# Values of the last block as seven half-size products instead of eight, all ahead of the eight heads; heads without value units

## The reference, cut to what matters

```python
def odd_mixer(hc, hl, w_in, decay_logit, w_out, need_ctx):
    q, k, v, g = split(h @ w_in, 4)          # h: 768 x 1024, w_in: 1024 x 4096
    ...                                      # axial rotation of q and k of the latents
    of, ob = retention forward, retention backward over chunks of 128 positions
    o = of + flip(ob)
    o = o * rsqrt(mean(o * o) + EPS)         # per head
    return (o * silu(g)) @ w_out             # latents only
```

## Time and profile before

| | us |
|---|---|
| median of 3 runs (lowest, highest) | 2440.76 (2439.26, 2443.21) |
| the profiled execution, its own time | 2440.05 |
| span of the profiled execution | 2438.8 |
| TensorE busy, of the span | 2294.6 (94%) |
| VectorE busy | 1731.1 (71%) |
| ScalarE busy | 641.6 (26%) |
| mean granted TensorE clock | 0.97 |
| last block from its first fold to the end | 2058 to 2439 |

### The profile page before, as it was taken

One profiled execution on the slowest core, in us unless ns is written; L12 is line 12 of the kernel. 1 busy time (PEld: TensorE's weight loads), 2 busy tenths in 40 slices (PEclk: granted clock), 3 DMA queues, 4 the chain that ended last, 5 costly groups with the idle time before them and its releaser, 6 DMA issues.

```text
span 2438.8 us, 40049 instructions
## 1 busy us (share of the span) xinstructions
PE 2294.6 (94%) x17170; PEld 1710.4 (70%) x17170; DVE 1731.1 (71%) x2924; ACT 641.6 (26%) x1321; POOL 236.2 (10%) x261
## 2 busy tenths in 40 slices
PE   7989989999997999999999989999897998999997
PEld 3676558888883788888756576675765754668973
DVE  3886477887798889878847969789797116774443
ACT  1314241111003311111043344444543312111111
POOL 2000000201541002024400000000000000000000
PEclk9999999999999999999999999999999898999998
DMA  8232335555432233343222101000010032112102
GB/s 336 88 120 88 129 112 173 173 172 171 162 126 77 88 130 130 130 147 133 94 89 83 37 23 36 12 30 22 19 36 20 2 119 76 67 65 70 35 18 103
DMA packets 42368, 227.93 MB, mean 93 GB/s; under 512 B 4752, under 2 KB 4880, under 8 KB 26064
## 3 DMA queue, kind: packets, MB, share of 16 engines
q1 hardware_dynamic: 21600, 140.56, 16.1%
q0 software_dynamic: 20016, 82.72, 10.0%
q10 hardware_dynamic: 576, 2.11, 0.2%
HBM read 219.07 MB, written 6.29 MB: 92 GB/s over the span
## 4 chain that ended last, share of the span: by engine, by line
PE 83%; DVE 12%; ACT 2%; issue 2%; DMA 1%; POOL 0%; ACTq 0%; DVEq 0%; POOLq 0%
PE ps L689 21%; PE ps L2302 10%; PE ps L911 7%; PE ps L3359 5%; PE ps L3549 3%; PE ps L2078 3%; PE ps L1045 2%; PE ps L461 2%; PE ps L1730 2%; PE ps L3744 2%; PE ps L2312 2%; PE ps L2321 2%; PE ps L1086 1%; PE ps L2990 1%; PE ps L3022 1%
## 5 line engine op out<-in xcount | busy, mean ns | idle before, releaser
L2302 PE MATMUL ps<-H,ring 128*128 128x256 f32 (+1 forms) x832 | 271.4, 487 | 5.4 <-ACT LW L2521 2.6
L689 PE MATMUL ps<-right_sums,left_sums 128*128 128x256 f32 x1056 | 242.8, 379 | 2.7 <-DVE left_sums L669 2.7
L2302 PEld LDWEIGHTS ps<-H,ring 128*128 128x128 f32 x832 | 157.4, 190 | 112.8 <-issue 92.8
L689 PEld LDWEIGHTS ps<-right_sums,left_sums 128*128 128x128 f32 x1056 | 200.5, 190 | 30.6 <-DVE left_sums L669 3.5
L689 PE MATMUL ps<-H,ring 128*128 128x256 f32 x704 | 164.2, 385 | 11.4 <-ACT H L632 11.4
L911 PE MATMUL ps<-G,ring 128*128 128x256 f32 x704 | 159.8, 379 | 0.0
L689 PEld LDWEIGHTS ps<-H,ring 128*128 128x128 f32 x704 | 134.6, 192 | 34.2 <-issue 11.5
L911 PEld LDWEIGHTS ps<-G,ring 128*128 128x128 f32 x704 | 133.8, 190 | 18.1
L381 POOL DMA_DIRECT2D ada_late<-ada_rest x104 | 55.9, 538 | 684.5 <-DVE mod L361 372.1
L756 ACT ACTIVATE C<-U,params_sb 128x512 f32<-128x512 f32 x44 | 35.8, 814 | 315.7 <-DVE U L781 315.7
L689 PE MATMUL ps<-H,left_sums 128*128 128x256 f32 x352 | 86.9, 388 | 0.0
(11 more groups left out here) (628 smaller groups left out, 4971.3 us busy)
## 6 DMA issues: line engine op xcount, KB each, us to landing
ada_late<-ada_rest POOLq DMA_DIRECT2D x104, 512.0 KB, 3.8
ring<-w_up SPq DMA_DIRECT2D x44, 1024.0 KB, 4.8
ring<-w_down SPq DMA_DIRECT2D x16, 1024.0 KB, 4.9
ring<-od_in SPq DMA_DIRECT2D x16, 1024.0 KB, 4.9
ring<-ev_in SPq DMA_DIRECT2D x15, 1024.0 KB, 4.8
ada_early<-ada_rest POOLq DMA_DIRECT2D x24, 512.0 KB, 4.8
ada_first_sb<-ada_first SPq DMA_DIRECT2D x7, 1024.0 KB, 16.4
ring<-ab_in SPq DMA_DIRECT2D x7, 1024.0 KB, 6.1
```

The costliest lines, as they stand in the source:

```text
L689: return pe.matmul(product(k, n, j), lhsT[:, i, :], rhs[:, i, :], start=(i == 0), stop=(i == 3))
L2302: mm = pe.matmul(k.ps[:, bank + b, 0:tn], wv[:, kk, (i % 2) * P:(i % 2 + 1) * P], k.H[:, kk, t0:t0 + tn], start=(kk == 0), stop=(kk == DT ...
```

## The change

Folds 11 to 16 are added for the values: folds 11 to 13 make columns 0 to 511 (slabs 12 and 13 together), folds 14 to 16 columns 512 to 1023 (slabs 14 and 15 together). In a fold the input blocks are the array's weights and the slab's blocks (two slabs side by side) the moving operand of 256 columns. All value units are removed; the six folds stand between the gates' folds and head 0. The output products that fill move to heads 3 to 7, always behind the states but for the last pair. The rest of the diff only routes the folds' outputs (`fold_out`: `k.V` for values) and adds the buffer `k.VL` over `k.XA`.

```diff
-FOLDS = [("q", 1), ..., ("g", 3)]
+FOLDS = [("q", 1), ..., ("g", 3)] + [("v", t) for t in range(6)]
...
+def value_fold_first_dve(k, q):
+    v, (A, S) = k.nc.vector, value_fold_left(k, q)
+    for h in range(2):
+        v.wait_ge(*k.when("slab", k.slab("od_in", 12 + 2 * q + h)))
+    v.wait_ge(*(k.when("fold", 13, 5) if q else k.when("fold", 9, 3)))
+    settled(k, v.tensor_tensor(S[0], A[1, 0], A[1, 1], ALU.add))
+    v.tensor_tensor(S[1], S[0], A[0, 0], ALU.subtract).then_inc(*k.says(DVE, "value fold left", q, 6))
+
+def value_fold_last_dve(k, q):
+    v, (A, S) = k.nc.vector, value_fold_left(k, q)
+    v.wait_ge(*(k.when("fold", 13, 7) if q else k.when("fold", 10, 3)))
+    v.wait_ge(*k.when("value fold left", q, 6))
+    v.tensor_tensor(S[3], A[0, 1], S[1], ALU.subtract).then_inc(*k.says(DVE, "value fold left", q, 3))
+    v.tensor_tensor(S[2], A[0, 0], A[1, 0], ALU.subtract).then_inc(*k.says(DVE, "value fold left", q, 7))
+
+def value_fold_pe(k, t):
+    q = t // 3
+    pe, m, (A, S) = k.nc.tensor, 11 + t, value_fold_left(k, q)
+    B, R = fold_right(k, "k")
+    def times(j, left, right):
+        for i in range(4):
+            mm = pe.matmul(fold_ps(k, m, j), right[:, i, (t % 3) * P:(t % 3 + 1) * P], left[:, i, :], start=(i == 0), stop=(i == 3))
+        mm.then_inc(*k.says(PE, "fold", m, j))
+    for h in range(2):
+        pe.wait_ge(*k.when("slab", k.slab("od_in", 12 + 2 * q + h)))
+    pe.wait_ge(*k.when("fold kept", m - 1))
+    times(1, A[0, 0], B[0, 0])
+    pe.wait_ge(*k.when("fold low", m - 1))
+    times(2, A[0, 1], B[1, 0])
+    pe.wait_ge(*k.when("value fold left", q, 6))
+    pe.wait_ge(*k.when("fold base", m - 1))
+    times(6, S[1], R[:, 1])
+    pe.wait_ge(*k.when("fold end", m - 1))
+    times(5, S[0], R[:, 0])
+    pe.wait_ge(*k.when("value fold left", q, 3))
+    times(3, S[3], B[1, 1])
+    pe.wait_ge(*k.when("value fold left", q, 7))
+    times(7, S[2], R[:, 2])
+    pe.wait_ge(*k.when("folded", m - 1))
+    times(4, A[1, 1], R[:, 3])
+    if t % 3 == 2:
+        for h in range(2):
+            k.mark(PE, "slab used", k.slab("od_in", 12 + 2 * q + h))
...
 def odd_gates_dve(k):
     for s in range(4):
         if s < 3:
             fold_left_dve(k, 8 + s)
+        else:
+            value_fold_first_dve(k, 0)
         axial_dve(k, ("od", "k"), k.Kr, TC, 2 * s)
         fold_base_dve(k, 7 + s)
...
         fold_ends_dve(k, 7 + s)
+    value_fold_last_dve(k, 0)
...
 def retention_scores_pe(k, h):
...
+    else:
+        pe.wait_ge(*k.when("fold base" if h == 0 else "folded", 16))
...
 def retention_states_pe(k, h):
-    pe.wait_ge(*k.when("value kept", NC * (h // 2) + NC - 1))
+    pe.wait_ge(*k.when("folded", 16))
...
-EARLY_PRODUCTS = {(6, 0): [(0, kk) for kk in range(4)], (6, 1): [(1, kk) for kk in range(4)], (6, 2): [(0, 4), (1, 4)], (7, 0): [(0, 5), (1, 5)]}
+EARLY_PRODUCTS = {(3, 2): [(0, 0), (1, 0)], (4, 2): [(0, 1), (1, 1), (0, 2)], (5, 2): [(1, 2), (0, 3), (1, 3)], (6, 2): [(0, 4), (1, 4)], (7, 0): [(0, 5), (1, 5)]}
...
 def retention_pe(k):
-    for u in range(NC):
-        value_unit_pe(k, u)
+    for t in range(6):
+        value_fold_pe(k, t)
...
 def retention_dve(k):
+    for t in range(6):
+        fold_base_dve(k, 11 + t)
+        if t == 2:
+            value_fold_first_dve(k, 1)
+        fold_ends_dve(k, 11 + t)
+        if t == 2:
+            value_fold_last_dve(k, 1)
```

More of the change, by code:

```diff
@@ L3296, in axial_dve @@
     v.tensor_tensor(x, x, rot, ALU.add).then_inc(*k.says(DVE, *what, "turned", j))
-FOLDS = [("q", 1), ("q", 2), ("q", 3), ("k", 0), ("k", 1), ("k", 2), ("k", 3), ("g", 0), ("g", 1), ("g", 2), ("g", 3)]
+FOLDS = [("q", 1), ("q", 2), ("q", 3), ("k", 0), ("k", 1), ("k", 2), ("k", 3), ("g", 0), ("g", 1), ("g", 2), ("g", 3)] + [("v", t) for t in range(6)]
 FOLD_FIRST = {"q": -1, "k": 3, "g": 7}
-FOLD_PART = {"q": (0, HALF, TC), "k": (4, 3 * P, 0), "g": (8, HALF, TC)}
+FOLD_PART = {"q": (0, HALF, TC), "k": (4, 3 * P, 0), "g": (8, HALF, TC), "v": (12, 2 * P, 0)}
 FOLD_ORDER = (1, 2, 6, 5, 3, 7, 4)
@@ L3382, in fold_pe, with fold_out @@
     k.mark(PE, "slab used", k.slab("od_in", fold_slab(m)))
+def fold_out(k, m, h, s):
+    what, n = FOLDS[m]
+    if what == "v":
+        return k.V[:, 3 * s + n % 3, (2 * (n // 3) + h) * 2 * P:(2 * (n // 3) + h + 1) * 2 * P]
+    w = FOLD_PART[what][1]
+    return {"q": k.Q, "k": k.Kr, "g": k.Gr}[what][:, 2 * n + h, s * w:(s + 1) * w]
 def fold_kept_act(k, m):
@@ L3396, in fold_base_dve @@
     what, s = FOLDS[m]
-    v, w, O = k.nc.vector, FOLD_PART[what][1], {"q": k.Q, "k": k.Kr, "g": k.Gr}[what]
+    v, w = k.nc.vector, FOLD_PART[what][1]
     p1, x0, x1, x2 = (k.FP[:, j, 0:w] for j in range(4))
@@ L3400, in fold_base_dve @@
     v.wait_ge(*k.when("fold", m, 2))
-    v.tensor_tensor(O[:, 2 * s, 0:w], p1, fold_ps(k, m, 2), ALU.add).then_inc(*k.says(DVE, "fold low", m))
+    v.tensor_tensor(fold_out(k, m, 0, 0), p1, fold_ps(k, m, 2), ALU.add).then_inc(*k.says(DVE, "fold low", m))
     v.wait_ge(*k.when("fold", m, 6))
@@ L3414, in fold_ends_dve @@
     v.wait_ge(*k.now(DVE))
-    v.tensor_tensor(O[:, 2 * s, w:2 * w], x1, fold_ps(k, m, 3), ALU.add).then_inc(*k.says(DVE, "fold high", m))
+    v.tensor_tensor(fold_out(k, m, 0, 1), x1, fold_ps(k, m, 3), ALU.add).then_inc(*k.says(DVE, "fold high", m))
     v.wait_ge(*k.when("fold", m, 7))
     settled(k, v.tensor_tensor(x2, x0, fold_ps(k, m, 7), ALU.add))
-    v.tensor_tensor(O[:, 2 * s + 1, w:2 * w], x2, fold_ps(k, m, 5), ALU.add).then_inc(*k.says(DVE, "fold end", m))
+    v.tensor_tensor(fold_out(k, m, 1, 1), x2, fold_ps(k, m, 5), ALU.add).then_inc(*k.says(DVE, "fold end", m))
@@ L3419, in fold_ends_dve, with value_fold_left @@
     v.wait_ge(*k.when("fold", m, 4))
-    v.tensor_tensor(O[:, 2 * s + 1, 0:w], x2, fold_ps(k, m, 4), ALU.add).then_inc(*k.says(DVE, "folded", m))
-    if what != "g":
+    v.tensor_tensor(fold_out(k, m, 1, 0), x2, fold_ps(k, m, 4), ALU.add).then_inc(*k.says(DVE, "folded", m))
+    if what in "qk":
         for n in range(2):
             k.mark(DVE, "od", what, "kept", 2 * s + n)
+def value_fold_left(k, q):
+    w = [k.slab_view("od_in", 12 + 2 * q + h, DT, 2 * P) for h in range(2)]
+    return {(h, e): w[h][:, e:DT:2, :] for h in range(2) for e in range(2)}, [k.VL[:, (j + 2) % 4] for j in range(4)]
@@ L3747 @@
 ODD_BANKS, ODD_SUM = (3, 7, 0, 1), 5
-EARLY_PRODUCTS = {(6, 0): [(0, kk) for kk in range(4)], (6, 1): [(1, kk) for kk in range(4)], (6, 2): [(0, 4), (1, 4)], (7, 0): [(0, 5), (1, 5)]}
+EARLY_PRODUCTS = {(3, 2): [(0, 0), (1, 0)], (4, 2): [(0, 1), (1, 1), (0, 2)], (5, 2): [(1, 2), (0, 3), (1, 3)], (6, 2): [(0, 4), (1, 4)], (7, 0): [(0, 5), (1, 5)]}
 def fill_pe(k, h, i):
     pe = k.nc.tensor
-    if NC + 3 * h + i < 4 * NC:
-        value_unit_pe(k, NC + 3 * h + i)
-        return
     for n, kk in EARLY_PRODUCTS.get((h, i), ()):
         pe.wait_ge(*k.when("slab", k.slab("od_out", 0)))
-        pe.wait_ge(*k.when("value kept", 4 * NC - 1))
         pe.wait_ge(*k.when("retained", kk))
         odd_product_pe(k, n, kk)
-def fill_act(k, h, i):
-    if NC + 3 * h + i < 4 * NC:
-        value_unit_act(k, NC + 3 * h + i)
 def retention_pe(k):
-    for u in range(NC):
-        value_unit_pe(k, u)
+    for t in range(6):
+        value_fold_pe(k, t)
     for h in range(RH):
@@ L3801, in retention_act @@
     log_exp_act(k)
-    for u in range(NC):
-        value_unit_act(k, u)
+    for t in range(6):
+        fold_kept_act(k, 11 + t)
     for h in range(RH):
@@ L3806, in retention_act @@
             retention_square_act(k, h - 1)
-        fill_act(k, h, 0)
         if h:
             retention_rstd_act(k, h - 1)
-        fill_act(k, h, 1)
-        fill_act(k, h, 2)
     retention_square_act(k, RH - 1)
@@ L3953, in lay_memory @@
     k.RL, k.RA = k.at("fold_right_latents", [P, 4, 4, HALF], values), k.at("fold_right_all", [P, 4, 4, 3 * P], LIMIT // 8 * 8 - 48 * P)
+    k.VL = k.at("value_fold_left", [P, 4, 4, 2 * P], xa)
     k.LF = [k.at(f"fold_left{n}", [P, 4, 4, P], xa + 2048 * n) for n in range(2)]
```

## The result

The changed kernel takes 2463.01 us (median of 4 runs, 2460.20 to 2463.99), the kernel before beside it 2441.99 (4 runs, 2439.26 to 2444.31): **21.0 us slower**, ratio 1.0086, 95% interval 1.0071 to 1.0101. The forecast was 2459.0, 18 us slower, with a range of 2452 to 2466.

A forecast was written before the change was run, and what follows sets the result against it. The prediction took TensorE's matmuls to limit the heads before the change. Its terms, -10.4 + 9.6 + 7.4 + 2.0 + 9.6 = +18.2 us, gave a median of 2459.0 us, with an 8-in-10 range of 2452 to 2466.

The forecast's parts named there:

- The work, -10.4: TensorE's value matmuls: 192 in units become 168 in folds, 24 fewer at 0.432 us each, -10.4 us.
- The seam at fold 11, +9.6: Before fold 11: 4.2 us for the load of slab 13 and 5.4 for VectorE's late sums, +9.6 us.
- the second wait of 1.5 us: In fold 11: TensorE, after product 6, waits again for VectorE's "fold end", about 1.5 us.
- 5.4: At fold 11: the part of the +9.6 us put down to what VectorE does late, 5.4 us.
- The seam at fold 14, +7.4: Before fold 14: slabs 14 and 15 wait for fold 13's end; 7.2 us plus 0.2 for semaphores, +7.4.
- The clock, +2.0: Behind the wait at fold 14: one stretch of some 4 us at half clock, +2.0 us.
- The heads, +9.6: Heads without filling: TensorE idles for walks, squares and head 0's decayed keys, together +9.6 us.
- The tail, 0: Behind the states of head 7: the tail stays the same, 0 us.
- VectorE is not late: Rival at fold 11: only the load counts, 4.2 in place of 9.6 us, 2453.6; chance 0.10.
- The loads come early: Rival at both seams: slabs come before folds 10 and 13 end, seams and clock cost nothing, 2440.0; chance 0.04.
- The waits of the heads are hidden: Rival in the heads: scores and squares overlap better and hide the waits, seams as forecast, 2449.4; chance 0.04.
- The clock falls more often: Rival: half clock also in fold 11's products 2 and 6 (3.5) and once in the heads (2.0), 2464.5; chance 0.17.

The follow-up runs named there:

- profile with filled heads: Changed kernel plus two extra matmuls of 512 columns, result unused, behind the states of heads 0, 1 and 2: 2461.56 us, ratio 1.0086.
- the first experiment: Changed kernel with VectorE's first two sums for the values behind the ends of fold 10 instead of ahead of key tile 6: 2457.53 us, ratio 1.0074.
- the matmuls put in it: Changed kernel with extra unused matmuls where TensorE waits for slabs, 5 ahead of fold 11 and 8 ahead of fold 14: 2459.13 us, ratio 1.0071.
- the one-pair run: Changed kernel without od_in slabs 14 and 15; folds 14 to 16 take slabs 12 and 13 again: 2451.96 us, ratio 1.0048.
- the run with both edits: Changed kernel with VectorE's first value sums behind the ends of fold 10 and without slabs 14 and 15: 2448.38 us, ratio 1.0033.
- the version with units: Against the kernel before: one-slab folds for slabs 12 to 14, slab 15 as six value units in heads 0 to 5: 2434.10 us, ratio 0.9975.

## Why the prediction was right, point by point

- **The work, -10.4**: right. The folds that nothing disturbs take 12.1 us each (12 and 13: 24.2).
- **The seam at fold 11, +9.6**: measured 10.0 (23.0 less 12.1 and the 0.9 of before), but made up otherwise. "TensorE does product 1 of fold 11 from 2225.3 to 2227.0" was too quick: it took 3.6 us at the low clock, beside VectorE's sums and so at no cost, as said. Then the clock was low again behind the wait, in products 2, 6 and the start of 5, 1.8 us, which the prediction had as a bound (3.5) and not in its sum; and this took the place of the second wait of 1.5 us, for "fold end". The profile with filled heads has it the other way round, full clock and a wait of 1.3, with the same end within 0.1. So the two do not add up, and the term came out near the forecast because VectorE's sums set it, not because the path on TensorE was foreseen. That VectorE's order matters is shown by the first experiment (3.8 us in the stretch), that it was less than 5.4 too.
- **The seam at fold 14, +7.4**: the wait was 7.7 us, from fold 13's end to the first product. The pair was in 7.3 us after the first issue.
- **The clock, +2.0**: 2.4 at fold 14, shown to be the wait's doing by the matmuls put in it, and gone with the loads in the one-pair run. The argument that a wait of 2.5 us leaves the clock full was weak, though. The earlier trace rows is the window of the wait itself (behind it the matmuls of the earlier trace rows did run at full pace); the changed kernel reads 1.00 there too, and 0.53 in the window behind. And the kernel before had a counterexample in its gates' folds, a wait of 2.45 us with low clock behind it. In the ten profiles this wait is 2.4 to 2.6 us long, and the product behind it takes 2.6 to 3.7 us in nine of them and runs at full pace in one, the run with both edits (first line before, second line that run):

```profile
2187.47 3.50 PE L3359 MATMUL ps<-fold_right_latents,fold_left 128*128 128x256 f32 x8 [2.45 <-DVE Gr L3418]
2185.08 1.99 PE L3359 MATMUL ps<-fold_right_latents,fold_left 128*128 128x256 f32 x8 [2.63 <-DVE Gr L3427]
```

- **The heads, +9.6**: mis-sized, and the largest of the errors; they took 76.7 where 75.0 was forecast, so the term is 11.3. The prediction gave the row sum 0.86 us; behind its wait for the square it takes 1.12, the same 0.27 that it did count for the output. Six heads wait so, 1.6 us. The first states stand behind a wait as well, for the decayed keys, and take 2.51 in place of 2.23. Heads 1 to 3 took 9.5 where 9.2 was forecast, heads 5 and 6 10.85 where "10 to 11" stood.
- **The tail, 0**: it is 70.6 us in place of 69.3 in this profile, because the clock fell behind the last walk. Whether the change has a part in this is not shown. In the nine profiles with a tail of this form it is 69.1 to 69.3 in five and 70.6 to 70.8 in four, each group with and without seams ahead; but all four have heads without filling, and the two profiles with heads filled throughout (the kernel before and the version with units) are among the five. The walk's wait of 2.5 us sometimes brings the low clock and sometimes not.
- **Together**: the stretch was to grow by 18.2 us and grew by 20.8. The misses are 0.4, 0.3, 0.4 and 1.7 (the heads), all the same way, so none of these terms hides another's error.

Of the rivals, *VectorE is not late* gave 2453.6 and is refuted by TensorE's wait of 2.2 us for a `Gr` sum and by the first experiment. *The loads come early* is refuted: slab 13 was issued 0.2 us behind fold 10's end. *The waits of the heads are hidden* is refuted by the chain. *The clock falls more often* is half right: it fell once more in fold 11's products, for 1.8 and not 3.5 us, and not in the heads. The Trainium skill ("TensorE: Matmul & The Clock Gate", section "HAM oscillation — how this bites in real kernels") has it that bursts of matmuls split by waits on a load can start at the low clock each time. The two waits on loads, of 4.9 and 7.5 us, agree. Behind the wait of 2.2 us on VectorE the clock was low here and full in the profile with filled heads (2.0 us); behind the heads' waits of 0.7 to 1.5 us nothing of it showed up to the states of head 7. The median, 2463.0, lies nearer to this rival's 2464.5 than to the forecast's 2459.0, but the rival's two terms do not make it: the low clock in products 2 and 6 takes the place of a wait, and the heads keep their clock. The miss in the heads is first matmuls behind waits.

## What to carry to other kernels

A step that needs two slabs of a two-slot ring at once puts a whole load on the critical path each time it comes to new ones; formed within one slab the same scheme kept 8.0 of its 10.4 us of work, and TensorE waited for no load. Work that stands in another chain's waits is worth more than its own time when it leaves: before moving it ahead, time the chain without it, from the rows of a place where nothing fills it (here head 7), and leave there as much as covers the waits. A wait for a transfer, placed in an in-order engine's list ahead of work that others need, delays all of that work; put it behind.

## What the runs showed of the hardware that was not expected

- A first matmul behind a wait costs more than the wait: the row sum 1.12 us instead of 0.86, the output 2.95 instead of 2.68, the first states 2.51 instead of 2.23, each time some 0.27.
- Two 1 MB loads issued 0.3 us apart landed 4.8 and 7.0 us after their issues, 7.3 for both from the first: the pair costs 2.4 us more than one, not twice.
- Keeping TensorE busy in a wait kept its clock at fold 14 (2.3 us) but gained nothing at fold 11, where the next wait, of 3.8 us, was followed by the low clock after all, and where VectorE's sums set the end.
- Waits of 2.0 to 2.6 us were followed by the low clock in some executions and not in others, at three places of the program: a gates' fold (low in nine profiles of ten), "fold low" of fold 10 (low in the changed kernel, full with filled heads) and the last walk (low in four of nine).
